# A retention, attention and expert trunk on one Trainium2 core: the first head's query and key projection made plain, in the order in which its data comes

## The reference, cut to what matters

```python
sh1p, sc1p, ... = ada_params(c_ctx[None, :], w_ada[i], b_ada[i])   # silu(cond) @ w_ada + b_ada
sh1s, sc1s, ... = ada_params(c, w_ada[i], b_ada[i])
hp = rmsnorm(xp, norm1[i]) * (1.0 + sc1p) + sh1p
hs = rmsnorm(xs, norm1[i]) * (1.0 + sc1s) + sh1s
q, k, v, g_f, g_b = jnp.split(h @ w_in, [hk, 2 * hk, 2 * hk + hv, 2 * hk + 2 * hv], axis=-1)
```

## Time and profile before

| what | us |
|---|---|
| median of 3 runs | 1774.48 (1773.4 to 1776.93) |
| span of the profiled execution | 1772.2 |
| TensorE matmul busy | 1684.3 |
| VectorE, ScalarE, GpSimd busy | 705.7, 260.4, 184.0 |

### The profile page before, as it was taken

How to read it: one execution, slowest core, us unless ns; L and a number is a source line. 1 busy time by engine, 2 the same in 40 slices (tenths; PEclk the granted TensorE clock), 3 DMA queues, 4 the chain that set the end, 5 groups by cost and what they waited for, 6 DMA issues and landing times.

```text
span 1772.2 us, 17375 instructions
## 1 busy us (share of the span) xinstructions
PE 1684.3 (95%) x6368; PEld 952.0 (54%) x6368; DVE 705.7 (40%) x1195; ACT 260.4 (15%) x554; POOL 184.0 (10%) x280
## 2 busy tenths in 40 slices
PE   5999999999999999999899999899999989999995
PEld 3864375644765465744464444354666654654442
DVE  1425533365333553255663232332233324533324
ACT  5100000000000000000121111322322321111111
POOL 2000100011000110001002222110000000022211
PEclk9999999999999999999999999999999999999998
DMA  8532561016410271103839999820000042579994
GB/s 320 204 142 95 199 224 48 0 48 235 156 47 0 95 286 57 47 0 141 256 149 307 351 339 329 273 100 3 22 25 11 0 120 95 201 244 343 340 329 143
DMA packets 159074, 280.21 MB, mean 158 GB/s; under 512 B 11396, under 2 KB 106392, under 8 KB 153896
## 3 DMA queue, kind: packets, MB, share of 16 engines
q1 hardware_dynamic: 144616, 236.39, 38.0%
q0 software_dynamic: 8960, 32.56, 7.0%
q10 hardware_dynamic: 5440, 10.49, 1.7%
HBM read 246.04 MB, written 33.37 MB: 158 GB/s over the span
## 4 chain that ended last, share of the span: by engine, by line
PE 79%; SPq 10%; DMA 4%; DVE 3%; issue 2%; ACT 2%; POOL 0%; DVEq 0%; POOLq 0%; ACTq 0%
PE banks L1085 11%; PE banks L1161 11%; PE banks L1060 8%; PE banks L1351 6%; SPq L659 5%; SPq L660 4%; PE banks L1482 4%; PE banks L1581 4%; PE banks L1157 3%; PE banks L1229 3%; PE banks L1368 2%; PE banks L1239 2%; PE banks L1217 2%; DMA wr<-in_moe_w_down 2%; PE banks L1513 2%; PE banks L1514 2%
## 5 line engine op out<-in xcount | busy, mean ns | idle before, releaser
L1351 PE MATMUL banks<-wr,arena 128*128 128x512 f32 x512 | 226.4, 595 | 10.8 <-DMA wr<-in_moe_w_down 10.1
L1161 PE MATMUL banks<-wr 128*128 128x512 f32 x432 | 191.4, 592 | 0.0
L1085 PE MATMUL banks<-wr 128*128 128x256 f32 x768 | 169.5, 379 | 0.0
L1351 PEld LDWEIGHTS banks<-wr,arena 128*128 128x128 f32 x512 | 94.6, 190 | 121.2 <-issue 118.9
L1085 PEld LDWEIGHTS banks<-wr 128*128 128x128 f32 x768 | 145.3, 190 | 22.7 <-issue 3.6
L1060 PE MATMUL banks<-wr,arena 128*128 128x512 f32 x320 | 143.4, 603 | 2.0 <-ACT arena L1688 2.0
L1161 PEld LDWEIGHTS banks<-wr 128*128 128x128 f32 x432 | 80.0, 190 | 91.2 <-issue 91.2
L1368 PE MATMUL banks<-wr,arena 128*128 128x512 f32 x256 | 115.4, 593 | 0.9 <-ACT arena L1804 0.9
L1060 PEld LDWEIGHTS banks<-wr,arena 128*128 128x128 f32 x320 | 60.5, 194 | 73.3 <-issue 72.3
L879 POOL DMA_INDIRECT acc_dram<-arena,put_ids x30 | 60.5, 2016 | 268.6 <-DVE arena L2363 268.6
L2348 DVE SCALAR_TENSOR_TENSOR arena<-banks,slot_w,arena 128x256 f32<-128x256 f32 x32 | 15.5, 484 | 173.6 <-ACT arena L1800 173.6
(11 more groups left out here) (324 smaller groups left out, 2193.7 us busy)
## 6 DMA issues: line engine op xcount, KB each, us to landing
wr<-in_w_ada SPq DMA_DIRECT2D x24, 2048.0 KB, 7.6
wr<-in_moe_w_gate SPq DMA_DIRECT2D x32, 1024.0 KB, 14.2
wr<-in_moe_w_up SPq DMA_DIRECT2D x32, 1024.0 KB, 16.3
wr<-in_moe_w_down SPq DMA_DIRECT2D x32, 1024.0 KB, 15.6
wr<-in_ret_w_in SPq DMA_DIRECT2D x12, 2048.0 KB, 14.0
wr<-in_ret_w_in SPq DMA_DIRECT2D x8, 1024.0 KB, 11.7
wr<-in_ret_w_out SPq DMA_DIRECT2D x4, 2048.0 KB, 7.7
arena<-mod_rows_dram SPq DMA_DIRECT2D x14, 512.0 KB, 6.4
```

Of the source, the lines that this page charges most:

```text
L1085: mm = mmul(dst[:, r * 256:r * 256 + 256], lhs, rhs, start=(start and r == 0 and k == 0), stop=(k == 3), skip_group_check=True)
L1161: mm = mmul(dst, X[X_OF[p]][:, k, cols], W[p][:, k, :], start=(k == 0 and p not in ("P2", "P7", "P3")), stop=(k == 3), skip_group_check=True)
L1351: mm = mmul(bank[2][:], xgT[:, e.par, k, :], expert_w(e.buf)[0][:, k].rearrange("p g f -> p (g f)"), start=(k == 0), stop=(k == KT - 1))
```

## The change

1. **Loads.** The tiles of x are issued by ScalarE, first of all that it does. SyncE issues chunks 0 and 2, the query and key weights of feature blocks 0 to 3, chunks 1 and 3, and, after the third chunk step, the query and key weights of blocks 4 to 7; the value weights wait for the first chunk step and the gates' for the eighth.
2. **ScalarE's order.** Silu and two copies first, then the squares; the decays, masks and query decays come after the chunks, and GpSimd trims the masks after that.
3. **Transposes.** All five tiles are transposed ahead of the chunks; evacuation is a plain copy of 128x512 on each of ScalarE and VectorE. Once a half of shift and scale is there, `hT` is modulated in place, a feature block at a time: VectorE over the 512 latent columns, ScalarE over the 128 prompt columns.
4. **Products.** `first_qk` replaces the Strassen form of the first head's query and key product: for each feature block k and each of four column blocks b, a 128x512 matmul into bank 4 + b and a 128x128 one into a quarter of bank 3, accumulated over k. Chunk steps 5 to 8 stand between its first blocks. ScalarE copies banks 4, 5 and 3, VectorE banks 6 and 7 (`first_copies`); VectorE steps its counter over the sums that are gone. The chunk steps take turns over three banks instead of four.

```diff
-PRE_SLOTS = (2, 3, 4, 1)
+PRE_SLOTS = (1, 2, 4, 3)
-T_BANK = {0: (4, 6, 0, 2, 4), 2: (0, 0, 0, 0, 0)}
+T_BANK = {0: (4, 6, 2, 0, 4), 2: (0, 0, 0, 0, 0)}
...
-            for t in FIRST_TILES:
-                src = a["x_prompt"][0] if t == PT else a["x_sample"][0, ORDER[t] * P:(ORDER[t] + 1) * P, :]
-                sp.dma_start(x[:, t, :], src).then_inc(S(f"x_back{t}"), 16)
-
-            for c in PRE_CHUNK_ORDER:
-                load_chunk(0, c, PRE_SLOTS[c])
+            def load_qk(half):
+
+                rows_of = slice(4 * half, 4 * half + 4)
+                for off, at in ((0, 0), (RH * DK, DK)):
+                    sp.dma_start(ring8(0)[:, rows_of, at:at + DK], w_ret[:, rows_of, off:off + DK])\
+                        .then_inc(S(f"ring_full{4 * half}"), 16)
+
+            for half, pair_of in enumerate(((0, 2), (1, 3))):
+                for c in pair_of:
+                    load_chunk(0, c, PRE_SLOTS[c])
+                if half:
+                    sp.wait_ge(S("proj_done"), PRE_ORDER.index(("part", 2)) + 1)
+                load_qk(half)
...
-                    if s == 1 and first:
-                        sp.wait_ge(S("proj_done"), PRE)
+                    if first and s < 3:
+                        sp.wait_ge(S("proj_done"), 1 if s == 1 else PRE)
...
+            def first_qk(slot):
+
+                w = ring8(slot)
+                for k in range(KT):
+                    if k % 4 == 0:
+                        pe.wait_ge(S(f"ring_full{k}"), full[k].next(2))
+                    pe.wait_ge(S("hTd"), NT + k + 1)
+                    pe.wait_ge(S("hTa"), NT + k + 1)
+                    for b in range(4):
+                        mm = mmul(bank[4 + b], w[:, k, tile_cols(b)], hT[:, k, 0:TS], start=(k == 0), stop=(k == KT - 1))
+                        if k == KT - 1:
+                            mm.then_inc(S("st_mm"), 1)
+                        mm = mmul(bank[3][:, tile_cols(b)], w[:, k, tile_cols(b)], hT[:, k, TS:T],
+                                  start=(k == 0 and b == 0), stop=(k == KT - 1), skip_group_check=True)
+                        if k == KT - 1:
+                            mm.then_inc(S("st_mm"), 1)
+                    for j in {0: (4,), 1: (5, 6), 2: (7,)}.get(k, ()):
+                        pre(j)
+
+            pe.wait_ge(S("set_a"), 3)
+            norm_T(0, xn[0])
+            pe.wait_ge(S("pick2_set"), 3)
+            for j in range(4):
+                pre(j)
...
+            def modulate_prompt(half):
+
+                act.wait_ge(S("modA"), half + 1)
+                act.wait_ge(S("hTa"), NT)
+                act.wait_ge(S("hTd"), NT)
+                for k in range(4 * half, 4 * half + 4):
+                    A_(hT[:, k, TS:T], hT[:, k, TS:T], ACT.Identity, scale=a1[:, 0, k, 1:2], bias=mod[:, 0, k, 1:2])\
+                        .then_inc(S("hTa"), 1)
+
+            for i in range(NT):
+                if i == 4:
+                    first_evac(0)
+                first_square(i)
+            for i in range(1, NT):
+                first_evac(i)
             for j, (kind, c) in enumerate(PRE_ORDER):
                 if kind == "part":
                     chunk_stage(j)
                 else:
                     chunk_evac(c, j)
-                for i in {3: (0,), 5: (1,), 7: (2, 3, 4)}.get(j, ()):
-                    norm_evac(0, 0, i)
+                if j % 4 == 3:
+                    modulate_prompt(j // 4)
+            decays()
...
+            def first_copies():
+
+                for b in range(2):
+                    act.wait_ge(S("st_mm"), 2 * b + 1)
+                    A_(qk4[:, 0, b, 0:TS], bank[4 + b], ACT.Copy).then_inc(S("st_a"), 1)
+                act.wait_ge(S("st_mm"), 8)
+                A_(qk4[:, :, :, TS:T], bank[3].rearrange("p (c j n) -> p c j n", c=2, j=2), ACT.Copy).then_inc(S("st_a"), 1)
...
+            def modulate(half):
+
+                dve.wait_ge(S("modA"), half + 1)
+                dve.wait_ge(S("hTa"), NT)
+                dve.wait_ge(S("hTd"), NT)
+                for k in range(4 * half, 4 * half + 4):
+                    v.tensor_scalar(hT[:, k, 0:TS], hT[:, k, 0:TS], a1[:, 0, k, 0:1], mod[:, 0, k, 0:1], ALU.mult, ALU.add)\
+                        .then_inc(S("hTd"), 1)
+
+            normalise(0)
+            for i in range(1, NT):
+                normalise(i)
+                first_evac(i - 1)
+            first_evac(NT - 1)
...
+            def first_copies():
+
+                dve.sem_inc(S("st_d"), len(ADDS) - 2)
+                for b in range(2, 4):
+                    dve.wait_ge(S("st_mm"), 2 * b + 1)
+                    v.tensor_copy(qk4[:, 1, b - 2, 0:TS], bank[4 + b]).then_inc(S("st_d"), 1)
```

More of the change, by code:

```diff
@@ L119, in gate_copy, with evac_no @@
     return h * 18 + (7 + GCOPIES.index(name))
-def swapped(n, i):
-    return int(n == 0 and i in (2, 3))
+def evac_no(n, t):
+    return n * NT + t + (KT + 1 if n else 1)
 def slices_done(h):
@@ L602, in head_loads @@
                     sp.wait_ge(S("st_mm"), gate_prod(h, "P6_1") - 32)
[L603 to L607, removed]
+                    for off in (0, RH * DK):
+                        dst = ring8(0)[:, :, 0:DK] if off == 0 else ring8(0)[:, :, DK:2 * DK]
+                        load(0, dst, w_ret[:, :, bass.ds(off + h * DK, DK)])
                 if not first:
@@ L815, in _ @@
             rstd(0)
+            pool.wait_ge(S("set_a"), 13)
+            mf, mb = mask[:, 0:4, :], mask[:, 4:8, :]
+            g.affine_select(out=mf, in_=mf, compare_op=ALU.is_ge, fill=0.0, base=0,
+                            pattern=[[0, 4], [1, P]], channel_multiplier=-1).then_inc(S("gset"), 1)
+            g.affine_select(out=mb, in_=mb, compare_op=ALU.is_ge, fill=0.0, base=0,
+                            pattern=[[0, 4], [-1, P]], channel_multiplier=1).then_inc(S("gset"), 1)
             def head(h, per):
@@ L960, in chunk_sum @@
                 for m in range(4):
-                    mm = mmul(bank[j % 4][:, 2 * m:2 * m + 2], stage[:, tile_cols(m)], pick2, start=True, stop=True)
+                    mm = mmul(bank[j % 3][:, 2 * m:2 * m + 2], stage[:, tile_cols(m)], pick2, start=True, stop=True)
                 mm.then_inc(S("proj_done"), 1)
@@ L1073, in products @@
             def products(h, f, slot):
-                first = isinstance(h, int)
                 B = w_blocks(f, slot)
@@ L1090, in products @@
                     pe.wait_ge(S("st_a"), copy_no(h, 0, "C11"))
-                elif not first:
+                else:
                     pe.wait_ge(S("st_d"), h * 32 + 4)
@@ L1096, in products @@
                     pe.wait_ge(S("st_d"), add_no(h, 0, "C21"))
-                if f == 0 and first:
-                    pe.wait_ge(S("hTa"), 4)
-                    pe.wait_ge(S("hTd"), 3)
                 if f == 0:
@@ L1111, in products @@
                 product("P2", False)
-                if f == 0 and not first:
+                if f == 0:
                     pe.wait_ge(S("ada_act"), h * 2 + 2)
@@ L1168, in head @@
                 slots_of = SLOTS_FIRST if first else SLOTS_LOOP
-                pe.wait_ge(S("ring_full0"), full[0].next(2))
-                products(h, 0, 0)
-                if not first:
+                if first:
+                    first_qk(0)
+                else:
+                    pe.wait_ge(S("ring_full0"), full[0].next(2))
+                    products(h, 0, 0)
                     out_proj(h, 1)
@@ L1652, in norm_evac @@
                     act.wait_ge(S("modA"), 2 * l + 1)
-                src = bank[T_BANK[n][i] + swapped(n, i)]
+                src = bank[T_BANK[n][i]]
                 for k in range(4):
@@ L1669, in router_copy, with first_square @@
                 A_(s_T[:, tile_cols(t)], bank[ST_BANK[l]][:, 0:P], ACT.Copy).then_inc(S("rt_copied"), 1)
[L1671 removed]
+            def first_square(i):
+                t = FIRST_TILES[i]
                 act.wait_ge(S(f"x_back{t}"), 16)
@@ L1969, in h_evac @@
                 dve.wait_ge(S("modA"), l + 2)
-                src = bank[T_BANK[n][i] + 1 - swapped(n, i)]
+                src = bank[T_BANK[n][i] + 1]
                 for k in range(4):
@@ L2112, in col @@
                     return tile[:, r * 4 + h:r * 4 + h + 1] if first else tile[:, bass.ds(h + r * 4, 1)]
-                product_sums(h, 0, 0)
-                if not first:
+                if first:
+                    first_copies()
+                else:
+                    product_sums(h, 0, 0)
                     op_evac(h)
```

115 lines of the change are left out of this document (56 added, 59 removed).

## The result

| kernel | median us | runs | profiled span |
|---|---|---|---|
| before | 1774.48 (1770.12 to 1776.93) | 5 | 1772.2 |
| after | 1780.45 (1777.42 to 1783.12) | 5 | 1777.0 |

The ratio is 1.0036, 95% interval 1.0019 to 1.0052: the change made the kernel slower, where I had forecast 1770.4 and a range up to 1774.6. TensorE's busy time is about the same as in the earlier trace rows.

What follows compares the result with a forecast made beforehand. TensorE, busy 95% of the span, was taken as the bound, with time to win only early. 29.2 + 40.3 + 1.7 + 0.85 = 72.05 against 76.17, 4.1 us less, gave 1770.4 us; range 1767.0 to 1774.6.

Steps and rivals of the forecast that it cites:

- yardstick: Start of the value products' P1, 76.17 us before, forecast 72.05; a lead there should reach the end whole.
- rival (e): Lead given back later, in the first head's adaLN slices or the experts' loads: 1774.5 us, 5%.
- V: Landing of the last small vector load, which starts the squares 1.05 later; taken as 7.5 us, bounds 6.1 and 14.0.
- rival (a): Small vectors held up behind x, landing near 10, losing 2.5 of the 4.1 us: 1772.9 us, 20%.
- counts for everything: Rival with the last vector landing at 14.0 because that landing decides all: 1776.9 us, 7%.
- The transposes: All five tiles transposed together, paced by TensorE at 1.79 a tile: 8.95 us; at most 0.7 less if the clock rises midway.
- The chunks' 1.9 and 6.4: Before the first projection: first chunk product 1.9 us, then 6.4 from its end to the first modulated write.
- the modulation: Modulating 128x512 in place ahead of the first projection: 0.4 us, upper bound 0.69.
- The plain product: First head's query and key product: 34.6 us, plus 5.7 for chunk products and sums inside it, together 40.3.
- Rival (c): Weight loads stick out by 78 ns after 64 narrow passes, 5.0 us: 1775.4 us, 6%.
- The seam: Value products' P1 waits for ScalarE's copy of bank 3 after the last pass: 0.85 us.
- The clock's fall of 1.7: One half-clock stretch of 3.4 us charged for gaps ahead of the first projection, costing 1.7 us.

Runs made afterwards that it cites:

- experiment 2: Kernel before with 108 idle semaphore increments at VectorE's start, loop at instruction 318: 1785.67 us, ratio 1.0061.
- experiment 10: Kernel after with the decay table's load issued last on its own semaphore, no padding, VectorE's loop at 190: 1778.53 us, ratio 1.0033.
- experiment 1: Kernel after with 20 idle semaphore increments at VectorE's start, loop at 210 as in the kernel before: 1770.57 us, ratio 0.9976.
- experiment 9: Kernel before with 112 idle semaphore increments at VectorE's start, loop at 322: 1774.63 us, ratio 1.0009.
- experiment 5: Kernel after with 20 increments of padding and the decay table's load issued behind the chunks on its own semaphore: 1767.39 us, ratio 0.9967.
- experiment 3: Kernel after with 20 increments of padding, x issued by SyncE behind the vector loads as before: 1770.1 us, ratio 0.9978.
- experiment 6: Kernel after with 20 increments of padding and all eight chunk steps ahead of the plain projection: 1773.18 us, ratio 1.0003.
- experiment 8: Kernel after with all chunk steps first, Strassen form kept, padding 11 on VectorE, and TensorE's loop moved by 16 to 511: 1772.2 us, ratio 0.9995.
- experiment 7: Kernel after with all chunk steps first, Strassen form kept, padding 11 on VectorE, TensorE's loop at 495: 1791.0 us, ratio 1.0083.

## Why the prediction was wrong

**The step that failed** is the yardstick's second half: "behind it both versions issue the same work, each load there waits for a TensorE or VectorE event, so a lead at 76.17 should reach the end whole". The instructions are the same, but not their place in VectorE's program. With the loop at instruction 190, VectorE stood for 3.44 and 3.08 us at the passes of heads 2 and 3, TensorE behind it, and at head 2 its clock fell as well; the prediction put this wait at nothing. My rival (e) allowed for a lead given back, but looked for it in loads of data, at 5%. Three pairs that differ by a few instructions without work show the cause: the kernel after against 20 increments (1.0036 to 0.9976), the same with the decay table apart (1.0033 to 0.9967), the kernel before with 108 against 112 (1.0061 to 1.0009). These are 0.5 to 0.7%, 9 to 12 us for two stalls. That the stall is a fetch of code is shown by six of them (the kernel after, experiments 2 and 10): in each a packet of queue 14 starts within the wait, and VectorE goes on 1.88 to 1.92 us behind its start. TensorE's starts account for 6.6 us in the profiled execution of the kernel after; its span is 8.4 over that of experiment 1. The rest comes between 850 and 1141 us, without a stall of this kind.

The yardstick was too strict there as well. Between 850 and 1141 us the difference to the kernel before moved by 1.4 later in the kernel after, 2.6 later in the run with 4 increments, 0.6 earlier in experiment 1 and 1.9 earlier in experiment 9. A lead at P1 reaches 850 us whole where nothing stalls, and the end only within some 3.5 us in a single execution (experiments 2 and 9). The measured time, over 1778, is an outcome to which I had given 0.07.

**V was mis-sized.** The last vector landed at 10.67, not 7.5, which is rival (a) (V near 10, 20%); it cost 3.2 us in the sum, and V past 9 was one of my own signs of being wrong. By the rule that I cited beside it, from the Trainium skill, "DMA: Bandwidth & Descriptors", section "Queues, rings and completion order", an engine leaves a ring only after a whole packet; the trace agrees in direction, with 7.27 us beside x against 2.78 ahead of it for the same transfer, but doesn't show packets as the reason. Experiment 5 parts it: without the table the six other vectors were there by 8.27, so 2.4 us of the 4.6 by which V was later than before (6.09) are the table's. That V "counts for everything" is refuted: experiment 3 gave 4.4 us of it back to a late chunk, experiment 5 made 2.45 us of it into 1.0 at P1.

**The transposes** took 7.40 us (14.78 to 22.18), not 8.95. They start every 0.213 us up to 19.07 and every 0.109 from 19.22 on, twice the pace, which I take for the rise of the clock midway that I had bounded at "0.7 less"; only the pace shows it, since the rows of the granted clock say 1.00 from 14 on. A tile's eight transposes then took 1.09, and the last two tiles started 1.29 apart (19.87 and 21.16), with VectorE's normalise and evacuation in turn as the limit. The chunks' 1.9 and 6.4 measured 1.92 and 6.45, the modulation 0.65 against 0.4. The first projection started at 31.20 instead of 29.2.

**The plain product**: forecast 34.6 and 5.7, together 40.3. The last pass starts at 71.55, and 0.11 later the next one could have: 40.46 us from 31.20, with no fall of the clock, 0.16 over the forecast; a wide pair and a narrow pair every 1.08 us. Rival (c), visible weight loads, is refuted: the narrow pairs take 0.22. The seam was 0.94 and not 0.85, since P1 starts 0.14 behind the copy's end. The moved work cost nothing, as forecast: ScalarE does it between 50 and 60 us, and TensorE is busy throughout.

**The clock's fall of 1.7** did not come in the kernel after and experiment 1 (1.00 from 28 to 34), but came in experiment 5 with the same gaps. It also came in experiment 10 and with 8 increments, where all up to the projection is as in the kernel after, and not with 4. So the charge was a coin's toss. The rule that I had set beside it, from the Trainium skill, "TensorE: Matmul & The Clock Gate", section "Why this matters for your kernels", that only far longer gaps matter, agrees with the kernel after and experiment 1, and not with experiment 5, whose longest gap was 1.57.

All in all P1 came at 72.60 against 72.05: errors of up to 3.2 us, V against the transposes and the clock, nearly cancelled. That the sum was right to 0.55 at the yardstick is luck, and so is the agreement of 0.9976, measured with the loop in its place, with my forecast of 0.9977. Two slips changed nothing: the first chunk's product ended at 24.17 and not 24.20, and the shares behind "faster" add up to 0.51, not 0.53.

**What the change is worth, part by part.** From experiments 1, 6 and 8, at P1: moving the chunk steps into the projection brings 4.5 us (77.22 to 72.69), the plain form that makes this possible costs 4.2 (35.6 against 31.4). These two cancel but for some 0.3 to 0.5 us. The lead of 3 us that remains over before with the Strassen form kept (experiment 8) is left for the other edits, the transposes ahead of the chunks and the decays behind them; none of these was undone by itself, and each figure is from one execution. In the time experiment 8 shows less of it (0.9995) than experiment 1 (0.9976). TensorE's loop begins at 511 in the one and at 476 in the other, and the difference isn't explained.

**Open.** Why VectorE stalls at 190 and 318 but not at 194, 198, 210 and 322, and how far the bad places reach below 190, I can't say. One reading fits all six places and is argued, not shown: the pattern comes back after 128 instructions, a packet has 8 KB, and a body of 263 instructions is 7 longer than two such blocks, so at a few of 128 starts it would touch one block more. The five packets in each pass of the kernel after, where experiment 1 has none, would then be a body that no longer stays loaded. For TensorE the place alone doesn't decide, since a loop at 495 stood in experiment 7 and not in the kernel before.

## What to carry to other kernels

A loop whose body is long can depend on where it begins in its engine's program: when an edit elsewhere changes the number of instructions ahead of it, compare idle time put down to "issue" and the packets of the instruction queues before and after the edit, and try the same kernel with a few increments of padding before holding the edit's own work to blame. A load that only a later stage needs should not sit on the semaphore that starts the first. And a plain product in the order of its data is worth what it lets run inside it, less its extra passes; work out both before choosing.

## What the runs showed of the hardware that I had not expected

- VectorE's code comes in packets of 8 KB on queue 14, TensorE's in 16 KB on queue 8. A loop of 263 instructions on VectorE ran its later passes either with no fetch of its own near the stall or with four within 20 us, five in the pass, and a stall of 3.1 to 3.4 us that ended 1.9 us behind the start of a packet, by its start (190 and 318 against 194, 198, 210 and 322). TensorE's stall of this kind was 9.05 us.
- A load that spreads 32 bytes over every partition, 4 KB in all, took 2.78 us ahead of x and 7.27 beside x on another queue; with x issued behind it, it had landed by 6.32 again.
- Two executions of the kernel before, without and with 112 increments, had the same first transposes and differed by 4 us at P1 by where the clock fell (76.17 and 80.2), while the medians agreed within 0.1%: a lead read from one profile is no better than that unless the windows of the clock agree too.
- TensorE doubled its pace in the middle of transposes alone, one every 0.213 us up to 19.07 and one every 0.109 from 19.22 on, while the rows of the granted clock read 1.00 throughout.
